# Half of the second MLP's up projection in seven block products for eight

## The reference

```python
h2 = rmsnorm(x, norm2_g[l])
x = x + jnp.square(jax.nn.relu(h2 @ w_mlp_in[l])) @ w_mlp_out[l]
return rmsnorm(x, final_g)
```

## Time and profile before

| what | value |
|---|---|
| time, median of 2 runs | 2980.11 us (2979.03 to 2981.2) |
| time of the profiled execution | 2981.11 us |
| its span, first to last instruction | 2979.4 us |
| TensorE busy | 2955.5 us, 99% |
| VectorE busy | 2013.4 us, 68% |
| ScalarE busy | 1730.2 us, 58% |
| mean granted TensorE clock | 0.997 |

### The profile page before, as it was taken

How to read it: one execution, slowest core, us unless ns; L and a number is a source line. 1 busy time by engine, 2 the same in 40 slices (tenths; PEclk the granted TensorE clock), 3 DMA queues, 4 the chain that set the end, 5 groups by cost and what they waited for, 6 DMA issues and landing times.

```text
span 2979.4 us, 37367 instructions
## 1 busy us (share of the span) xinstructions
PE 2955.5 (99%) x13294; PEld 2429.6 (82%) x13294; DVE 2013.4 (68%) x2103; ACT 1730.2 (58%) x2453; POOL 493.1 (17%) x422
## 2 busy tenths in 40 slices
PE   9999999999999999999999999999999999999998
PEld 7887888888888888888877778888888888888887
DVE  6667654566667777676779996655566666666666
ACT  6776645547655555555665666554557555555555
POOL 1000110110034243320247660110000000000000
PEclk9999999999999999999999999999999999999999
DMA  7656666656666666666756555666666666666664
GB/s 244 183 156 179 202 193 203 199 183 200 194 192 220 194 219 192 222 220 196 253 183 199 178 184 180 209 207 211 204 203 186 199 196 191 194 192 193 194 190 162
DMA packets 298828, 588.43 MB, mean 198 GB/s; under 512 B 18448, under 2 KB 18464, under 8 KB 298336
## 3 DMA queue, kind: packets, MB, share of 16 engines
q1 hardware_dynamic: 292336, 563.61, 61.2%
q0 software_dynamic: 5952, 22.77, 2.4%
q10 hardware_dynamic: 432, 0.62, 0.1%
HBM read 574.35 MB, written 12.58 MB: 197 GB/s over the span
## 4 chain that ended last, share of the span: by engine, by line
PE 92%; DVE 4%; issue 1%; ACT 1%; DMA 1%; POOL 0%; SPq 0%; DVEq 0%; ACTq 0%
PE banks L1691 92%; DVE wlo L1095 2%; DMA raw<-in_w_in 1%; ACT whi L602 1%; DVE W L1488 0%; DVE W L1480 0%; PE banks L1694 0%; DVE banks L1481 0%; DVE banks L1483 0%; ACT L602 0%; ACT W L602 0%; ACT G L602 0%; DVE W L1348 0%; POOL W L508 0%; SPq L387 0%
## 5 line engine op out<-in xcount | busy, mean ns | idle before, releaser
L1095 DVE TENSOR_TENSOR wlo<-raw,whi 128x1024 fp32r<-128x1024 f32 x1048 | 1393.7, 1335 | 884.9 <-ACT whi L602 878.1
L602 ACT ACTIVATE whi<-raw 128x1024 fp32r<-128x1024 f32 x1048 | 1107.2, 1060 | 1052.9 <-PE banks L1691 939.7
L1691 PE MATMUL banks<-whi,Y 128*128 128x512 f32 x4800 | 1484.6, 389 | 0.3 <-DVE W L1176 0.2
L1691 PEld LDWEIGHTS banks<-whi,Y 128*128 128x128 f32 x4800 | 901.1, 188 | 188.2 <-issue 0.9
L1691 PE MATMUL banks<-wlo,Y 128*128 128x512 f32 x2400 | 933.7, 389 | 0.0
L1691 PE MATMUL banks<-whi,XH 128*128 128x512 f32 x1792 | 708.7, 395 | 14.5 <-DVE wlo L1095 14.5
L1691 PE MATMUL banks<-whi,XL 128*128 128x512 f32 x1792 | 699.6, 390 | 0.0
L1691 PE MATMUL banks<-wlo,XH 128*128 128x512 f32 x1792 | 699.5, 390 | 0.0
L1691 PEld LDWEIGHTS banks<-wlo,Y 128*128 128x128 f32 x2400 | 450.6, 188 | 93.1
L1691 PEld LDWEIGHTS banks<-whi,XH 128*128 128x128 f32 x1792 | 337.3, 188 | 96.8 <-issue 15.3
L1691 PEld LDWEIGHTS banks<-whi,XL 128*128 128x128 f32 x1792 | 337.2, 188 | 72.0
(11 more groups left out here) (252 smaller groups left out, 1220.0 us busy)
## 6 DMA issues: line engine op xcount, KB each, us to landing
raw<-in_w_in SPq DMA_DIRECT2D x384, 512.0 KB, 4.0
raw<-in_w_mlp_up SPq DMA_DIRECT2D x128, 512.0 KB, 4.0
raw<-in_w_mlp_down SPq DMA_DIRECT2D x128, 512.0 KB, 3.7
raw<-in_w_mlp_in SPq DMA_DIRECT2D x128, 512.0 KB, 3.8
raw<-in_w_mlp_out SPq DMA_DIRECT2D x128, 512.0 KB, 3.7
raw<-in_w_branch SPq DMA_DIRECT2D x80, 512.0 KB, 4.3
raw<-in_w_out SPq DMA_DIRECT2D x64, 512.0 KB, 4.4
tables<-G POOLq DMA_DIRECT2D x8, 1024.0 KB, 8.3
```

The lines of the kernel that those rows point to most:

```text
L602: return nc.scalar.activation(out_, in_, f, **kw)
L1095: tt(wlo[:, i % RING, :], raw[:, i % RING, :], whi[:, i % RING, :].bitcast(F32), ALU.subtract)\
L1691: return nc.tensor.matmul(out_, l, r, start=start, stop=stop, **kw)
```

## The change

Chunks 2 to 15 of the up projection are taken in 7 groups (g = 1 to 7) of two chunks, 1024 hidden columns. Of these, 256 columns of each chunk (512 in all) are computed by Strassen's scheme in the form with seven products: the 256 positions are cut in two halves of 128, the 2048 input rows in two of 1024, the 512 columns in two of 256. Seven products of blocks, instead of eight, are made and combined by additions. The other 256 columns of each chunk are computed plainly.

The loops over `body(j)` on all engines are replaced, in the second MLP, by a written out list `stream` of units: **F** (a product unit: 4 row blocks of a 256 column weight block or sum of blocks, 12 matmuls of 128x256), **U** (a plain up unit of 4 row blocks by 256 columns, 24 matmuls of 128x256) and **D** (a down unit, as before). A group is 14 F, 5 D, 8 U and 11 D; the first has 4 D in both places, and the eighth is 8 D. So the 7 products come in two sevens (`q` = 0 and 1, each 512 of the 1024 rows that a half has). A seven uses four weight blocks: `B11`, `B21`, `B22` and `T3`, loaded by four transfers of 512 KB into `W` and `G` in place of `raw` units, and four sums of them which VectorE forms (`t_sum`), so that the seven operands are `B11, B21, B22, T1, T3, T2, T4`. Each is then split as any unit. The bytes loaded are the same as before.

The input's sums (`form_step`, ten operations, and four low parts, `form_lo`) are formed once, in the first chunk. After a group's products `combine` makes the outputs from the seven sums in seven operations on 128x256. Hidden values are moved in pieces of 32x128 (`half_moved`), and squared, transposed and split at the first four F of the next group (`chunk_square`, `chunk_turned`, `chunk_lo`). In the first block some semaphores are renamed and shared; its order is unchanged.

```diff
@@ names and placement (plan)
-            counts["dve"] += NF * NCH
+            counts["dve"] += NF * NCH if b == 1 else 4 * (NF // 2 + 2)
...
+        FIRST_ORDER = "FFFFFFFFFFFFFFDDDDUUUUUUUUDDDD"
+        ORDER = "FFFFFFFFFFFFFFDDDDDUUUUUUUUDDDDDDDDDDD"
+        stream = []
+        for g in range(1, NF // 2 + 1):
+            kinds = FIRST_ORDER if g == 1 else ORDER if g < NF // 2 else "D" * 8
+            stream += [(kind, g, kinds[:p].count(kind)) for p, kind in enumerate(kinds)]
+        unit_at = {entry: GROUP0 + p for p, entry in enumerate(stream)}
...
+        PLACE = [(4, 0), (5, 0), (7, 0), (6, 0), (6, 1), (4, 1), (5, 1)]
+        P1, P2, Q3, Q5, P7, P6, Q4 = (banks[:, bk, T * e:T * e + T] for bk, e in PLACE)
+        B11, B21, B22, T1, T3, T2, T4 = FORM = [slot(W, 10), slot(W, 11), slot(W, 12), slot(W, 13), slot(G, 0), slot(G, 1), slot(G, 2)]
@@ sync: loads
+                    if kind == "F" and i % 7 == 0:
+                        q = i // 7
+                        if (g, q) == (1, 0):
+                            sp_.wait_ge(S("combined"), COMBINE)
+                        else:
+                            sp_.wait_ge(lo_done, unit_at["F", g, 6] + 1 if q else unit_at["F", g - 1, 13] + 1)
+                        for to, k, c in ((B11, 4 * q, c0), (T3, 4 * q, c0 + CH), (B22, 8 + 4 * q, c0 + CH), (B21, 8 + 4 * q, c0)):
+                            sp_.dma_start(to.rearrange("p (k n) -> p k n", n=T), up[:, k:k + 4, c:c + T]).then_inc(S("quad_in"), 16)
@@ scalar
+                def half_moved(g, s, c, first):
...
+                    for m in range(first, first + 8):
...
+                        ins = a(dst[:, :, 2 * s:2 * s + 2, tq, :], src[:, :, :, fq, :], ACT.Relu)
@@ vector
                     for i in range(7, 14):
                         lo(base, i)
+                        if first and b == 2:
+                            for n in range(2 * (i - 7), 2 * (i - 7) + 2):
+                                if n < 10:
+                                    form_step(n)
+                                else:
+                                    form_lo(n - 10)
                     add(base, 0)
...
+                def t_sum(q, n):
+                    if n == 0:
+                        dve.wait_ge(S("quad_in"), 64 * (q + 1))
+                    if n >= 2:
+                        dve.wait_ge(S("t_sums"), 4 * q + (1, 3)[n - 2])
+                    to, x, y = ((T1, T3, B11), (T3, T3, B22), (T2, T1, B22), (T4, T2, B21))[n]
+                    tt(to, x, y, ALU.add).then_inc(S("t_sums"), 1)
+                def unit_lo(kind, g, i):
...
+                    q, f = 2 * (g - 1) + i // 7, i % 7
+                    if f < 4:
+                        t_sum(q, f)
+                    dve.wait_ge(hi_done, u_ + 1)
+                    tt(wlo[:, u_ % RING, :], FORM[f], whi[:, u_ % RING, :].bitcast(F32), ALU.subtract).then_inc(lo_done, 1)
+                def strassen():
+                    for p, (kind, g, i) in enumerate(stream):
+                        unit_lo(kind, g, i)
...
+                        if p >= 4 and stream[p - 4][0] == "D":
...
+                                down_add(d // per)
+                        if g < NF // 2 and GROUP0 + p == unit_at["F", g, 13] + 4:
+                            combine(g)
+                        if g > 1 and kind == ("F" if g < NF // 2 else "D") and i < 4:
+                            (chunk_square, chunk_lo)[i // 2](2 * g - 2 + i % 2)
+                            if i < 2:
+                                chunk_turned(2 * g - 2 + i)
@@ tensor
+                def unit_form(g, i):
...
+                    for k in range(4):
...
+                        for n, (l, w) in enumerate(((lh, whi), (lh, wlo), (ll, whi))):
+                            ins = mm(banks[:, bank, T * e:T * e + T], l, w[:, u_ % RING, T * k:T * k + T],
+                def unit_half(g, i):
...
+                    for k in range(4):
+                        for t in range(NT):
+                            for n, (l, w) in enumerate(((YH, whi), (YH, wlo), (YL, whi))):
+                                ins = mm(banks[:, bank, T * t:T * t + T], l[:, 4 * (i // 2) + k, P * t:P * t + P], w[:, u_ % RING, T * k:T * k + T],
```

More of the change, by code:

```diff
@@ L369, in _, with n_of, strassen_loads @@
         def _(sp_):
+            def n_of(view):
+                return view.shape[-1]
             def load(base, i, view):
-                if not (isinstance(base, int) and base + i < RING):
+                if isinstance(base, int):
+                    n = raw_slot[base + i]
+                    if n >= RING:
+                        sp_.wait_ge(lo_done, raw_units[n - RING] + 1)
+                    i = n
+                else:
                     sp_.wait_ge(lo_done, base + (i - RING + 1))
-                sp_.dma_start(raw[:, i % RING, :].rearrange("p (k n) -> p k n", n=CH), view)\
+                sp_.dma_start(raw[:, i % RING, :].rearrange("p (k n) -> p k n", n=n_of(view)), view)\
                    .then_inc(raw_in[i % RING], 16)
+            def strassen_loads(up, dn):
+                for i in range(8):
+                    load(MLP2, 8 + i, up[:, UK * i:UK * i + UK, CH:2 * CH])
+                for i in range(8):
+                    n, k = i // 2, UK * (i % 2)
+                    load(MLP2, 16 + i, dn[:, k:k + UK, CH * n:CH * n + CH])
+                for kind, g, i in stream:
+                    c0 = 2 * CH * g
+                    if kind == "F" and i % 7 == 0:
[6 more added lines that the diff above has]
+                            sp_.dma_start(to.rearrange("p (k n) -> p k n", n=T), up[:, k:k + 4, c:c + T]).then_inc(S("quad_in"), 16)
+                    elif kind == "U":
+                        k, c = 4 * (i // 2), c0 + CH * (i % 2) + T
+                        load(0, unit_at[kind, g, i], up[:, k:k + 4, c:c + T])
+                    elif kind == "D":
+                        n, chunk, half = down_of(g, i)
+                        k = 4 * chunk + UK * half
+                        load(0, unit_at[kind, g, i], dn[:, k:k + UK, CH * n:CH * n + CH])
             def tables():
@@ L416, in _ @@
                     load(mlp_base(b, NF - 1), i, dn[:, k:k + UK, CH * n:CH * n + CH])
+            for i in range(8):
+                n, k = i // 2, 4 * (NF - 1) + UK * (i % 2)
+                load(LAST2, i, rows("w_mlp_out_2")[:, k:k + UK, CH * n:CH * n + CH])
             for by, n, t, lo_, hi_ in OUT_PARTS:
@@ L1016, in mlp @@
                     hi(base, i)
+                    if b == 2 and i >= 10:
+                        form_hi(2 * (i - 10))
                 for i in range(4):
@@ L1019, in mlp @@
                     hi(base, 12 + i)
+                    if b == 2 and i < 2:
+                        form_hi(2 * i + 1)
+                if b == 2:
+                    strassen()
+                    st["hi"] = LAST2
+                    return
                 with act.Fori(1, NF - 1) as j:
@@ L1756, in lru @@
                     if f:
[L1757 removed]
+                        pe.wait_ge(S("lru_pre"), f)
                     else:
@@ new lines, in strassen @@
+                def strassen():
+                    for kind, g, i in stream:
+                        if kind == "F":
+                            unit_form(g, i)
+                        elif kind == "U":
+                            unit_half(g, i)
+                        else:
+                            n, chunk, half = down_of(g, i)
+                            if i == 0:
+                                pe.wait_ge(S("hidden_split"), chunk0(2) + (2 * g if g < NF // 2 else NF - 1))
+                            per = down_units(g) // 4
+                            if i % per == 0:
+                                pe.wait_ge(evict["dve"], e0 + 4 * g + n - 1)
+                            unit(0, unit_at[kind, g, i], YH, YL, KD + 4 * (chunk % 2) + UK * half, PA[n % 2], i % per == 0, i % per == per - 1)
```

259 lines of the change are left out of this document (220 added, 39 removed).

## The result

The changed kernel takes 3155.01 us (median of two runs, 3154.12 and 3155.91), the kernel before 2980.11: 1.0587 times as long, 95% interval 1.0557 to 1.0618. The profiled execution took 3154.12.

A forecast was written before the change was run, and what follows sets the result against it. The prediction took TensorE, busy 99% of the span, as the bound. To the profiled 2981.1 us it added 121 for six steady groups, 35 for the stage's ends and 7 for the clock, less 1: 3143 us, range 3085 to 3220.

The forecast's parts named there:

- TensorE, columns saved: TensorE, per group: 360 matmuls of 256 columns at 0.1165 us replace 192 of 512 columns, a gain of 1.6 us.
- Second half of the products: Second seven of each group: blocks requested late, TensorE stalls 9.1 us, then 2.7 of VectorE pacing; 11.8 us a group.
- First half: First seven of each group: VectorE's list makes TensorE wait at units 2 to 5, 8.5 us a group (5 to 11).
- Plain half and down units: Units beside ScalarE's 64 smaller moves of hidden values: about 1.5 us a group (0 to 4).
- Ends of the stage: First chunk's input forms 7 us, group 1 19, second group 4, last down stretch 5: 35 us together.
- Clock: Products behind the 9 us stall run at half speed: some 1 us a group, 7 us in all (0 to 35).
- A steady group: Each of six groups loses 20.2 us, 121 together; its window 107 us where two chunks took 87.
- (a): Rival: the ring of four units ahead covers VectorE's work, TensorE alone sets the end, 2969 us; chance 0.04.
- (b): Rival: one of the two stalls is hidden, 8 us a group less, 3085 to 3110 us; chance 0.08.
- (c): Rival: 1 KB packets cost by count (+45) or half clock throughout the products (+28), 3180 to 3220 us; chance 0.15.
- (d): Rival: narrow matmuls are bound by weight loads at 0.188 us each, +124, 3267 us; chance 0.04.

The follow-up runs named there:

- e4: The kernel before, with the second MLP's up units in its 15 bodies cut into 256-column matmuls, each with its own weight load: 2999.0 us.
- e6: The changed kernel, with the plain half of a pair's up projection in matmuls of 512 columns instead of two of 256: 3145.8 us.
- e1: The changed kernel, with the second seven's four blocks in buffers of their own and requested together with the first seven's: 3095.0 us.
- e2: The changed kernel, with VectorE squaring and turning a pair of hidden chunks during the last four down units of the group before: 3129.6 us.
- e5: e1 plus the next group's blocks requested earlier, and the first seven's sums, squares and turns done among the down units before: 3064.3 us.
- e9: e5 with VectorE's list spread further over the group, three more buffers for sums and both sets of blocks requested earlier: 3054.7 us.
- e11: e10 with ScalarE's chunk_hi moved behind the sixth and ninth products, the first group's blocks requested later, and three other places changed: 3024.2 us.
- e7: The changed kernel, with VectorE adding the first down result before the last two input-form steps in the first body, not after: 3154.9 us.
- e10: e9 plus e6's 512-column plain half, and the input forms made from the first body's second unit instead of its seventh: 3039.6 us.
- e3: The changed kernel with 30 extra 512-column matmuls on data at hand, ahead of the wait before each group's second seven: 3154.9 us.
- e8: The kernel before, with the up units of the second MLP's 15 bodies in 128-column matmuls, each with its own weight load: 3298.8 us.
- e12: e11 with the eight block sums of a group left out (output not the reference's) and ScalarE's moves spread over eight units: 2995.6 us.

## Why the prediction was right, and where its terms were off

Forecast 3143 us, range 3085 to 3220, slower; measured 3155, 12 above. By its own steps:

- **TensorE, columns saved** (1.6 us a group): mis-sized. A 256-column matmul with full weights takes 0.120 us, not 0.1165, so 360 of them are 43.2 us against 43.5: the gain is 0.3 us. The step took its number from matmuls with narrow weights. e4 and e6 agree at 13.6 and 13.7 ns for each extra matmul. So the fixed price of matmuls half as wide eats the columns saved, and all else is loss; at the forecast gain it would have been 11 us against a loss of 175.
- **Second half of the products** (stall 9.1, then 2.7 of pacing): right in mechanism and size. The blocks landed 8.4 to 8.7 us after their request in three of the four steady groups (8.6 forecast) and 10.8 in the fourth. The Trainium skill ("DMA: Bandwidth & Descriptors", Anatomy of one DMA) gives its fit for one transfer on GpSimd's path; for four on SyncE's queue it would make 6.8 us, an estimate, and the measured 8.4 decides against using it so. The seven stalls are 9.0, 9.9, 6.6, 6.8, 9.1, 6.9 and 8.7 us, mean 8.1. e1 took them away and gave 60.0 us back. The seven units behind the stall took 12.85 us for 10.1 of full speed, 2.8 over (2.7 forecast). That the time of packets does not go by their count is shown by the page of the profile: queue q1 has 321008 packets where it had 292336, the same 563.61 MB, and 55.9% of 3152 us instead of 61.2% of 2979. In the group shown the blocks in 1 KB packets landed 1.5 us apart, the units in 2 KB packets behind them 1.35.
- **First half** (8.5 a group): right in mechanism, a little too small. The first blocks landed 11.5 to 12.2 us after the conversion that they wait for, not 10, so VectorE started 3.1 to 3.8 us ahead of TensorE and not 4.9, and the fifth product started 14.9 to 15.6 us behind the first (14.1 forecast). The waits at the second, third, fourth and fifth product are 2.1, 3.1, 1.8 and 1.0 us in the group from 2547 on, 8.0 in all. e2 gave 25.4 of the 28 us that its operations count. It is VectorE's list in front, and behind it a second limit that the step didn't see: ScalarE's chunk_hi, which holds the third product's copy until the last down unit is done. It has a part in the 47 us by which e5 missed and in the 33 of e9, but not all: of e11's 15, which moved it together with four other places, 7.0 came in the products of five groups, and the larger part in the first body. What chunk_hi alone is worth was not measured.
- **Plain half and down units** (1.5): the pieces took 0.268 us (0.27 forecast). The waits are 0.4 and 0.5 us at two down units and 0.4 at a plain one; with the slower starts around them the down units of a steady group take 45.0 us for 43.5 and the plain ones 23.5 for 23.0, 2.0 over.
- **Ends of the stage** (first body 7, last down stretch 5): 7.3 and 4.7. Group 1 took 81.9 us where some 84 were forecast: its first seven waited 1.1 us, not 5. e7 confirms that the first body's wait is the length of the list and not its order; e10, which starts the list earlier, still has 5.4 us there, behind e9's early request for blocks; in e11, which also moves that request, the longest wait of the first body is 1.2.
- **Clock** (1 a group): too high, and in the wrong place. Behind the long stalls e3 leaves 0.2 us at most, because VectorE's 2.27 us a unit stands beside the half clock. At the head of a steady group half clock lasts 10.2 us as well (window 2553.40:2563.60 at 0.50), where waits of 1 to 3 us alternate with single units; but TensorE is in no link of the chain there, and the load of the second seven makes it wait behind that stretch anyway. Behind the first body's stall 14 matmuls of 512 columns start 0.427 us apart, 3 us in all, with the chain again on VectorE and the loads. Only in the last down stretch does the chain run through TensorE behind a stall; eight starts up to 0.43 apart cost 1.7 us there (3.4 us at 0.52 in the window below). The wait of "2.6 of 5 us" in the prediction is 2.4: 2.60 is the busy time.

```profile
3099.70:3103.10 3.40, 3.40 (x9) 2.68 (x10) 3.40 (x4) 0.00 (x0) 0.00 (x0) 0.52 0.69 233
```

- **A steady group**: 107 us forecast and 1 of clock; the three windows above have 110.5 in the mean. By TensorE's starts four steady groups have 110.2: 41.7 in the products (39.9 forecast, the rest being the first blocks' later landing and the one slow second set), and 68.5 in down and plain units (67.4 forecast, 0.7 of the rest being the 192 narrow matmuls there). These are readings of the trace; no run took the two parts apart. That the sum fell only 12 us short is in part luck: 3 us a steady group too little, against the clock's 7 and group 1's head too much.
- **Rivals**: (a) and (b) fell, both stalls are there at nearly full size; (c) fell, neither the packets' number nor a half clock throughout the products appeared; (d), narrow matmuls bound by weight loads at 0.188, is refuted by 0.120; a floor shows one width lower, at 0.112 (e8).

## What to carry to other kernels

A scheme that saves products gains little where the products that remain are half as wide: here 6.2% fewer columns in half as wide pieces saved 0.3 us of 43.5, and 1.6 with the plain half in wide ones. With the sums left out altogether e12 only reached the time of the kernel before. When a unit of TensorE becomes half as long, every engine that feeds it needs its lead counted anew in units of the new length, and each instruction on it that waits for an old unit is to be moved behind those that needn't. Where two limits lie on the same units (a half clock and VectorE's pace, a list and a wait in another engine's queue), their costs don't add, and taking one away shows the other.

## What was unexpected in the hardware

- TensorE's price for one matmul with new 128 x 128 weights: 0.227 us for 512 columns, 0.120 for 256, 0.112 for 128. Down to 256 columns it is the columns and 13.6 ns; below there is a floor near 0.11, which is also how close the weight loads start.
- Matmuls on data at hand, issued into a wait, kept the granted clock at 1.00 behind it (e3), at no gain in time, because another engine set the pace.
- Four transfers of 512 KB asked for together landed one after the other, 3.8, 5.4, 6.9 and 8.4 us after the first request, though four more were asked for right behind them; the windows that hold them have 366 to 370 GB/s, while the whole group's mean was 153: a late request, not the rate, made the stall (e1).
